# Opening of a two-layer encoder kernel: one modulation slot loaded ahead of x, a third slot summed on TensorE

## The reference, cut to what matters

```python
def _modulation(c, w_mod, b_mod):
    m = jax.nn.silu(c) @ w_mod + b_mod          # (1, 1024) @ (1024, 3072)
    shift, scale, gate = jnp.split(m, 3, axis=-1)
    return shift[:, None, :], scale[:, None, :], gate[:, None, :]

for i in range(2):
    shift, scale, gate = _modulation(c, w_mod[i], b_mod[i])
    h = _rmsnorm(x, norm_g[i]) * (1.0 + scale) + shift
    y = short_conv_mixer(h, ...) if i == 0 else spatial_gating_mixer(h, ...)
    x = x + gate * y
return _rmsnorm(x, final_g)
```

## Time and profile before

| | before |
|---|---|
| median of 3 runs (lowest, highest) | 815.83 us (815.69, 815.84) |
| profiled execution: its time, its span | 815.77 us, 813.6 us |
| TensorE, VectorE, ScalarE, GpSimd busy | 803.5, 649.0, 442.6, 51.0 us |
| granted TensorE clock, mean | 0.999 |

### The profile page before, as it was taken

How to read it: one execution, slowest core, us unless ns; L and a number is a source line. 1 busy time by engine, 2 the same in 40 slices (tenths; PEclk the granted TensorE clock), 3 DMA queues, 4 the chain that set the end, 5 groups by cost and what they waited for, 6 DMA issues and landing times.

```text
span 813.6 us, 15228 instructions
## 1 busy us (share of the span) xinstructions
PE 803.5 (99%) x5618; PEld 752.7 (93%) x5618; DVE 649.0 (80%) x950; ACT 442.6 (54%) x624; POOL 51.0 (6%) x68
## 2 busy tenths in 40 slices
PE   9999999999999999999999999999999999999996
PEld 8779999999999999988889888899999999988896
DVE  5989999999999999898653687567888888897534
ACT  4575656565666666562333844446667676763220
POOL 1010000000000000000000000010000000000000
PEclk9999999999999999999999999999999999999999
DMA  9995566667565656687422263414455445487103
GB/s 350 367 243 134 152 183 178 188 173 195 168 203 161 206 162 198 169 321 286 151 79 78 66 246 102 130 27 143 142 155 155 130 128 154 131 310 256 52 1 104
DMA packets 39502, 137.85 MB, mean 169 GB/s; under 512 B 4272, under 2 KB 6448, under 8 KB 39472
## 3 DMA queue, kind: packets, MB, share of 16 engines
q1 hardware_dynamic: 32128, 111.16, 37.8%
q0 software_dynamic: 6912, 25.17, 16.4%
q10 hardware_dynamic: 432, 1.13, 0.4%
HBM read 108.09 MB, written 4.19 MB: 138 GB/s over the span
## 4 chain that ended last, share of the span: by engine, by line
PE 93%; DVE 3%; DMA 1%; issue 1%; ACT 1%; SPq 0%; POOL 0%; DVEq 0%; ACTq 0%; POOLq 0%
PE pp L1186 11%; PE pp L1187 11%; PE pp L1188 11%; PE pp L1042 8%; PE pp L1043 8%; PE pp L1044 8%; PE p_aux L1186 7%; PE p_aux L1188 7%; PE p_aux L1187 7%; PE pp L1322 4%; PE pp L1323 4%; PE pp L1324 4%; PE p_aux L1396 2%; PE pp L1141 1%; DVE acc_s L1482 1%; DMA raw_s<-in_stream 1%
## 5 line engine op out<-in xcount | busy, mean ns | idle before, releaser
L1186 PE MATMUL pp<-h_hi,wh 128*128 128x256 f32 x280 | 79.3, 283 | 0.0
L1188 PE MATMUL pp<-h_hi,wl 128*128 128x256 f32 x280 | 79.2, 283 | 0.0
L1187 PE MATMUL pp<-h_lo,wh 128*128 128x256 f32 x280 | 79.2, 283 | 0.0
L1693 DVE TENSOR_TENSOR wl<-wt,wh 128x1024 fp32r<-128x1024 f32 x56 | 66.5, 1218 | 0.2 <-ACT wh L697 0.2
L697 ACT ACTIVATE wh<-wt 128x1024 fp32r<-128x1024 f32 x56 | 59.0, 1055 | 13.7 <-DVE wt L1674 7.6
L1186 PE MATMUL pp<-s_hi,wh 128*128 128x256 f32 x224 | 63.4, 283 | 0.0
L1187 PE MATMUL pp<-s_lo,wh 128*128 128x256 f32 x224 | 63.4, 283 | 0.0
L1188 PE MATMUL pp<-s_hi,wl 128*128 128x256 f32 x224 | 63.4, 283 | 0.0
L1188 PE MATMUL p_aux<-s_hi,wl 128*128 128x256 f32 x224 | 63.4, 283 | 0.0
L1186 PE MATMUL p_aux<-s_hi,wh 128*128 128x256 f32 x224 | 63.4, 283 | 0.0
L1187 PE MATMUL p_aux<-s_lo,wh 128*128 128x256 f32 x224 | 63.4, 283 | 0.0
(11 more groups left out here) (237 smaller groups left out, 2598.0 us busy)
## 6 DMA issues: line engine op xcount, KB each, us to landing
raw<-in_stream SPq DMA_DIRECT2D x144, 512.0 KB, 4.1
wl<-raw POOLq DMA_DIRECT2D x28, 512.0 KB, 4.5
raw_l<-in_stream SPq DMA_DIRECT2D x18, 512.0 KB, 4.9
raw_s<-in_stream SPq DMA_DIRECT2D x16, 512.0 KB, 13.7
wl_b<-raw POOLq DMA_DIRECT2D x16, 512.0 KB, 4.5
raw_m<-in_stream SPq DMA_DIRECT2D x14, 512.0 KB, 3.3
x_s<-in_xt SPq DMA_DIRECT2D x4, 512.0 KB, 5.9
w_lo_s<-raw POOLq DMA_DIRECT2D x4, 512.0 KB, 5.3
```

Of the source, the lines that this page charges most:

```text
L1186: pe.matmul(out, hi, hi_of(k), start=fresh and k == 0, stop=False, skip_group_check=not fresh)
L1187: pe.matmul(out, hi, lo_of(k), start=False, stop=False, skip_group_check=not fresh)
L1188: mm = pe.matmul(out, lo, hi_of(k), start=False, stop=k == 3, skip_group_check=not fresh)
L1693: dve.tensor_tensor(wl[par][:, part], wt[par][:, part], f32(wh[par][:, part]), ALU.subtract).then_inc(t_cut, 1)
```

## The change

The first modulation slot is transferred ahead of x, and left out at its old place. Its direct sums start after 16 keep-clock products in place of 28, and 18 more keep-clock products follow them ahead of the sums of squares. The third slot of group 0 goes to `direct_columns`, in place of the three keep-clock products ahead of the broadcast; VectorE is left with one slot (two tiles) of four. The variance comes first on VectorE after the additions.

```diff
-WARM = (28, 3, 2)
+WARM = (16, 0, 2)
+WARM_X = 18
...
-S_DIRECT = (2, 1, 0, 0)
+S_DIRECT = (3, 1, 0, 0)
...
+            sp.dma_start(raw_s[:, 0, :], stream[0, :, :]).then_inc(ms_in[0], 16)
             for k in range(4):
                 sp.dma_start(x_s[:, 2 * k:2 * k + 2, :], xt[:, 2 * k:2 * k + 2, :]).then_inc(x_in[k], 16)
             for q, what in enumerate(START_ORDER[:Q_RING]):
+                if q == 0:
+                    continue
...
             keep_clock(WARM[0])
             pe.wait_ge(wide_ready, 1)
             direct_columns(0, 0)
+            keep_clock(WARM_X)
             pe.wait_ge(sq_added, SQ_START)
...
             direct_columns(0, 1)
-            keep_clock(WARM[1])
+            direct_columns(0, 2)
             broadcast(p_rstd[:, :], 2, ALL)
...
-            start_tiles(0, 4)
             dve.wait_ge(stat_sum, 1)
             rsqrt(1, p_rstd[:, 0:NCH], 1.0 / D, NCH)
-            start_tiles(0, 5, 6)
+            start_tiles(0, 6)
```

## The result

The changed kernel takes 817.78 us (median of 11 runs, 817.63 to 819.69) against 815.80 us before (11 runs, 815.64 to 816.05): 1.98 us more, a ratio of 1.0028 with a 95% interval of 1.0020 to 1.0035. The interval lies above 1, so it is slower, by a little over the 0.2% that the forecast took as its bound. The profiled execution has a span of 815.8 us (813.6 before) and took 818.00 us.

The account below looks back on a forecast made before the run. TensorE bounds the kernel, and the broadcast's start paces the opening. Sums at 13.58, then 0.90 and twice 1.78, put the broadcast at 18.04, 1.93 us later: 815.77 + 1.93 = 817.70, given as 817.7 us, range 816.9 to 818.3.

Parts of the forecast that it names:

- The path: In the opening, TensorE's list leads through the sums and two direct slots to the broadcast, at 18.04 instead of 16.11.
- prices of the pairs: On TensorE in the opening, each pair of weight load and matmul takes 0.111 us, direct or keep-clock.
- the start of the sums: TensorE's sums of squares start at 13.58 us instead of 12.40, within bounds of 13.58 to 13.7.
- The body has no slack: From 90 to 800 us TensorE is busy 709.43 of 710 us, so a later opening counts in full.
- The tile in the chain of waits: VectorE's third-slot tile at 13.11, ahead of the variance at 13.52; claimed to hold it up by next to nothing.
- From the sums to the broadcast: On TensorE: sums 0.90 us, second and third slots 1.78 each, so the broadcast starts at 18.04.
- The diagonals: Ready 3.71 us after the sums start, at 17.29, hidden behind the third slot's sums ahead of the broadcast.
- VectorE's two tiles: Two tiles fewer on VectorE, 1.60 us, only lengthen its idle time ahead of the scaling of x.
- The first slot ahead of x delays the additions by 1.1 us: x's first pair lands at 6.70 instead of 5.35, so VectorE's additions end at 13.37 instead of 12.26.
- rival 4: x later still in the opening, delaying sums, direct slots and broadcast by half a microsecond more: 818.2 us; chance 0.14.
- 0.52 us to spare: All of TensorE's slack ahead of the broadcast: 0.36 us waiting for the diagonals and 0.16 for the first slot.

Follow-up runs that it names:

- experiment 3: Changed kernel with eight more keep-clock products (16 pairs) ahead of the broadcast: 819.70 us.
- experiment 6: Kernel before with the variance ahead of VectorE's first tile, two tiles behind it and two behind the diagonals: 815.82 us against 815.80.
- Experiment 1: Kernel before with only the third slot's sums moved to TensorE, without the three keep-clock products ahead of the broadcast, transfers in old order: 816.62 us against 815.86.
- Experiments 2: Kernel before with only the first slot transferred ahead of x and the keep-clock products split 16 and 18: 817.01 us against 815.86.
- experiment 8: Changed kernel with ten instead of eighteen keep-clock products between the first slot's sums and the sums of squares: 819.36 us.

## Why the prediction was right

The forecast was slower, at 817.7 us; measured were 817.78. The path and the prices of the pairs were right. One term, the start of the sums, was too small in the traces, and the median came out as close as it did with some luck.

- *The body has no slack, so the opening counts in full.* Shown by the table, and by experiment 3.
- *The tile in the chain of waits held up the variance by next to nothing.* Shown by experiment 6: 0.01 us.
- *From the sums to the broadcast: 0.90 and twice 1.78.* Measured 0.89 and 3.58. The diagonals hid behind the third slot, as forecast, with 1.2 us in hand instead of 0.75; GpSimd's power took 1.03 us instead of 1.45 (below).
- *VectorE's two tiles shorten nothing.* Its idle time grew to 2.01 us, where over 1 was forecast. Experiment 1 shows the same with x in its old place.
- *The first slot ahead of x delays the additions by 1.1 us; TensorE's list decides, sums at 13.58.* This is the term that was mis-sized: the sums started at 13.85 to 13.91 in the three traces, beyond the bounds of 13.58 to 13.7 that the prediction gave. Two things are off, and each was taken from one execution as if fixed. The first pair of x landed at 6.9 to 7.2, not 6.70, so that the additions end between 13.5 and 13.9; that is up to 1.85 us behind its old 5.35, where the prediction took 1.35 as the most. And the first 16 keep-clock products end anywhere between 6.95 and 8.04, against 7.79 worked out, so that in one trace TensorE's list decides and in two the additions. Experiments 2 and 3 have the same lists up to the sums: there they start at 13.35, held by the additions, and at 13.92, held by TensorE's list. The wait of TensorE ahead of the sums (0.95 and 1.07 us) is the sign that the prediction named for rival 4, x later still: it was at work in part, with some 0.3 of its 0.5 us in the profiled execution (818.00 against 817.70). By the median the sum held, 817.78 against 817.7; that is in part luck, since the three profiled executions (818.00, 818.00, 818.03) all lie 0.2 us above the median and none shows the sums at 13.58.
- *A pair costs 0.111 us in the new place as well.* Measured 0.112 in experiments 1 and 3. The 81 ns that the Trainium skill (TensorE: Matmul & The Clock Gate, section Back-to-back issue gap) gives for such a stream is not reached in any stretch of such pairs shown here; by that figure, as an estimate, the 40 pairs from the sums to the broadcast would take 3.2 us and experiment 1 would have cost nothing.
- *The order of the list settles it.* The change asks TensorE for 22 more pairs ahead of the broadcast, where it had 0.52 us to spare, to relieve an engine that waited there anyway. The ten behind the sums lost 0.76 us (experiment 1). The twelve ahead of them lose time only in executions where TensorE's list reaches the sums after the additions; in the others the later x holds the sums back, by 1.1 us (experiment 8) to 1.5 (13.91 against 12.40).

## What to carry to other kernels

A chain of waits names one parent of each step; before work is moved off that parent, the start of the other parents has to be worked out, since a second one may end within a hundredth of a microsecond of it. Moving work from an engine with idle time to the one whose list leads to the next release is a loss as soon as the work is longer than what that list has to spare (0.36 us ahead of the broadcast here, against 1.11 for ten pairs), and it is found by counting that engine's list between its fixed points. Where a forecast rests on two paths that end within a few tenths of each other, the spread between executions decides which of them ends last, so several traces of the same program are worth more than a finer sum from one.

## What the runs showed of the hardware that was not expected

- **An idle gap of TensorE cost more than the gap.** In experiment 8 TensorE was busy up to 12.1, idle 1.40 us, busy again at 13.50, and at 14.3 the granted clock fell to 0.50 for 3.4 us. In two traces of the changed kernel gaps of 0.95 and 1.07 us were followed by a granted clock of 1.00 throughout the opening. Of its 30 timed runs, three took 819.65 to 821.55 us, with a mean granted clock of 0.994 to 0.996 over the execution against 0.998 to 1.000 in the others; that these three, and the three of experiment 2, are the same fall behind a gap is likely but not shown, as none of them was profiled.
- **The first stretch of TensorE runs at half the pace, and its length differs from execution to execution.** In the trace before, keep-clock pairs took 0.213 us until 7.0 us and 0.111 behind that. In the eleven traces the change of pace comes between 5.3 and 7.8 us, with the first work at 1.67 to 1.68 in each, and that alone moves the end of the first 32 pairs of the changed kernel (6.95 to 8.04). Stretches of the profile read a granted clock of 1.00 in both parts, but the clock's own record in each trace begins only within 0.1 us of the change of pace, with 1.00; ahead of it there is none. In experiment 8 pairs under a granted clock of 0.50 took 0.213 us as well, so the first stretch has the pace of the lower level (1.2 GHz). Why its length differs is not shown.
- **GpSimd's power -1/2 of 128x4 numbers took 1.45 and 1.40 us** where VectorE made two `SCALAR_TENSOR_TENSOR` tiles beside it (before, and experiment 2), and 1.03 to 1.13 us where it made none or one (the other nine traces). No run tested this by itself.
- **The first transfer was not a fixed price.** The slot that went first landed 3.9 us after its issue, the pair of x that went first before took 4.6; the next one landed 2.5 us behind it instead of 1.35.
